# Gates and p's product of a two-block model as split products, with the waits around them reordered

## The chip, the cores and the metric

The kernel runs on one core of one Trainium2 chip. It is written in Bass: each of the five instruction streams (TensorE = PE, VectorE = DVE, ScalarE = ACT, SyncE = SP, GpSimd = POOL, the last unused) is written out by hand, and they meet only through semaphores. The metric is the device time in microseconds (us), the median of several runs; lower is better.

## The reference, cut to what matters

Two blocks run one after the other on x, 256 positions by 2048 channels, in float32. The first has two layers; each projects the normed x to 6668 columns, sends them through three mixers (sliding window attention over 12 heads, a conformer convolution, a gated delta rule), gates the results y and adds `y @ w_out` to x. The second has two layers as well: a pool mixer in layer 0, a recurrent unit (LRU) in layer 1. The parts that the change touches are these:

```
# attention of a layer of the first block, per head h
s = q k^T / 8, masked; p = softmax([s, sink]);  o = p v;  y[0:768] = o * silu(za)
# LRU: uc = causal conv of u over 4 positions, 16 heads of 256 channels
r  = sigmoid(uc_h @ wa_h + ba);  ig = sigmoid(uc_h @ wx_h + bx)
# end of both layers of the second block
x = x + rmsnorm(o) * g_post
gate = sigmoid(rmsnorm(x) @ w_ple_gate);  e = p[i] @ w_ple      # p[i]: 256 x 256
x = x + rmsnorm(e * gate) * g_ple_out
```

## The kernel before

**Weights.** All weights lie in one array in the order of use, in chunks of at most 128 x 2048 float32 (1 MB). `plan()` makes the list. SP loads chunk c into `W[c % 5]` once chunk c - 5 is used up. A chunk named in `SPLIT` is taken apart: ACT copies it, rounded to fp32r, into `WH[s % 4]` (`high`, L991), once the split chunk four before it is used up; DVE writes the rest, W - WH, over the chunk itself as `WL` (`low`, L1658). The inputs are held the same way as an upper and a low part (`HH`, `HL` for the first block's h and y). A split product is three fp32r matmuls: WL by the upper part, WH by the low part, WH by the upper part. In mode "wide" the last two are one matmul of 512 columns, so a k-tile is four matmuls of 256 columns and four of 512. The LRU's gate weights (`lru_w`, eight chunks) and `w_ple_2` (two chunks a layer) are not in `SPLIT`: their products are plain float32 matmuls, straight from `W`.

**Order on the engines.** Each engine walks the same list of chunks. On ACT and DVE a `tick` runs `high(c + 3)` or `low(c + 3)` first and then four `pump`s; PE runs four `pump`s spread over the k-tiles of a chunk. A pump moves every side task (a Python generator) on by one `yield`, so `rest(n)` puts n pumps between two steps of a side task. `group(n)` is n ticks and then a wait for the last chunk of them; `finish` runs a side task to its end. Each engine runs its own stream in order, so a wait holds back all that is behind it. `lag` says how many of the engine's own earlier instructions may still be under way.

**Attention.** It is a side task on PE (L743 ff.), ACT (L1210 ff.) and DVE (L1947 ff.), begun at the start of the projection of za. Heads are taken in three lots q of four: `scores(q)` on PE writes four PSUM banks; on DVE it scales and masks each into `AS`, takes the maxima and signals `mx`; on ACT it takes the exponentials and signals `es`; `weights(q)` on DVE divides by the sum and signals `p`; `turned(q)` transposes three banks on PE, which ACT and DVE copy back to `AS`; last comes `av` (three banks), multiplied by silu(za) into Y on DVE. The four side banks of PSUM go round in a fixed order: `turned(0)` and `turned(1)` write banks that the first three DVE operations of `scores(1)` and `scores(2)` set free. With PE's chunks after the start of attention named Z1 to Z4 (za, pumps 1 to 16), P (17 to 20), A (21 to 24), B (25 to 28), G1 (k-tiles 10 to 13 of y, 29 to 32), G2 (6 to 9, 33 to 36), G3 (14 and 15, 37 to 40), G4, G5, G6 (the same k-tiles for the next 512 output columns, 41 to 52) and G7 (k-tiles 0 to 3), the steps stand at these pumps:

```
              PE   ACT  DVE          after: PE   ACT  DVE
scores(0)     22   26   19                  22   26   22
weights(0)              27                            30
scores(1)     30   34   27 (behind weights) 30   34   30
turned(0)     32   32   29                  32   32   32
weights(1)              35                            38
scores(2)     38   42   35                  38   42   38
turned(1)     40   40   37                  40   40   40
silu(za)           43                            43
weights(2)              43                            46
turned(2)     48   48   45                  47   47   47
av            52        49                  50        50
X back (DMA)       52                            50
```

After B both ACT and DVE leave the side tasks for a moment: DVE scales the last part of Y (`scaled`), ACT and DVE write upper and low parts of y's k-tiles 6 to 9, 14 and 15 (`ysplit`), which G2 and G3 read. Those of k-tiles 0 to 5 come after `finish(att)`.

**End of a layer of the second block.** `out_part(l, 3)` adds the last part of the output product to O in four column groups i; DVE adds (after `low` of the tick), ACT sums the squares, DVE multiplies by g_post. `post(l, n)` then takes the total, ACT the inverse root, and DVE adds O to X in eight operations. On PE, `post` runs four groups of p's product and after each but the first transposes a quarter of X (`turn`), whose copies become the upper and low parts of the next h.

**LRU.** In step n, PE projects z(n) and u(n + 1), then runs `gates(n)`: 16 matmuls of 256 columns over uc, in two halves (r and ig). `conv(n)` on DVE and `first_tap(n)` on ACT make uc as side tasks. Eight chunks of the output product stand between u(3) and `gates(2)`, between u(5) and `gates(4)`, and behind `gates(6)`.

## Time and profile before

| | us |
|---|---|
| median of 3 runs | 2449.18 (2449.09 to 2449.77) |
| profiled execution, whole | 2449.32 |
| its span, first to last instruction | 2447.5 |
| PE busy | 2414.6 (99%) |
| DVE busy | 1657.7 (68%) |
| ACT busy | 1250.9 (51%) |
| mean granted PE clock | 0.997 |
| DMA, mean | 175 GB/s, 48% of the 16 engines |

A line of the timeline reads: start, duration, engine, line, operation, output <- input, shapes, count, and in brackets the engine's idle time before it with what ended it. L421 is the helper `mm`, L991 `high`, L1658 `low`; L977, L1623 and L1627 are the helpers of all other ACT and DVE work. A plain float32 matmul shows as two records. Matmul durations overlap: the time of one is the distance between starts.

### The profile page before, as it was taken

How to read it: one execution, taken by the hardware profiler on the slowest of the kernel's cores; microseconds unless marked ns; L12 is line 12 of the kernel's file. 1: busy time of each engine (PE TensorE's matmuls, PEld its weight loads, DVE VectorE, ACT ScalarE, POOL GpSimd, SP SyncE). 2: the span in 40 equal slices, each digit the busy share in tenths (PEclk: the TensorE clock that was granted, in tenths of full speed). 3: DMA queues.
4: the chain of work that ended last, by engine and by line, in shares of the span. 5: the costliest groups of instructions: out<-in, count | busy, mean ns of one | idle time of the engine just before them, and what ended most of it. 6: DMA issues, size and time to landing. Idle time of an engine off the chain costs nothing.

```text
span 2447.5 us, 34157 instructions
## 1 busy us (share of the span) xinstructions
PE 2414.6 (99%) x14580; PEld 2139.5 (87%) x14580; DVE 1657.7 (68%) x1895; ACT 1250.9 (51%) x1378; POOL 0.2 (0%) x4
## 2 busy tenths in 40 slices
PE   8999999999999999999999999999999999999997
PEld 8999988899999888988888888878888888888876
DVE  5788758557887585667657577565657667667764
ACT  5554256455543565544444344456556465565573
POOL 0000000000000000000000000000000000000000
PEclk9999999999999999999999999999999999999999
DMA  6543223555532335555555555555454555555553
GB/s 235 207 175 137 98 109 130 198 206 199 182 138 90 118 130 198 195 189 189 189 189 189 189 189 189 194 206 191 153 186 179 193 183 189 189 177 185 203 193 121
DMA packets 63977, 428.17 MB, mean 175 GB/s; under 512 B 7121, under 2 KB 7249, under 8 KB 14801
## 3 DMA queue, kind: packets, MB, share of 16 engines
q1 hardware_dynamic: 61280, 414.97, 47.6%
q10 hardware_dynamic: 2544, 11.01, 1.2%
q8 instruction: 115, 1.88, 0.3%
q14 instruction: 38, 0.30, 0.0%
HBM read 421.76 MB, written 4.19 MB: 174 GB/s over the span
## 4 chain that ended last, share of the span: by engine, by line
PE 97%; DVE 1%; ACT 1%; issue 0%; DMA 0%; DVEq 0%; SPq 0%; ACTq 0%
PE PS L421 95%; PE PS L547 1%; PE PS L652 1%; DVE X L1627 0%; PE PS L643 0%; PE PS L785 0%; ACT Q L977 0%; ACT WH L991 0%; PE PS L766 0%; DVE SM L1642 0%; DVE Q L1627 0%; DVE O L1623 0%; DMA W<-in_wall 0%; DVE H L1623 0%; DVE Y L1623 0%
## 5 line engine op out<-in xcount | busy, mean ns | idle before, releaser
L1658 DVE TENSOR_TENSOR WL<-W,WH 128x2048 fp32r<-128x2048 f32 (+2 forms) x392 | 860.4, 2203 | 505.7 <-ACT WH L991 505.3
L991 ACT ACTIVATE WH<-W 128x2048 fp32r<-128x2048 f32 (+2 forms) x392 | 718.0, 1842 | 506.4 <-PE PS L421 421.1
L421 PE MATMUL PS<-H,WH 128*128 128x256 f32 (+1 forms) x4864 | 946.5, 327 | 0.0
L421 PEld LDWEIGHTS PS<-H,WH 128*128 128x128 f32 x4864 | 713.0, 191 | 43.9
L421 PE MATMUL PS<-H,WL 128*128 128x256 f32 x3392 | 558.3, 284 | 7.6 <-DVE H L1627 7.6
L421 PEld LDWEIGHTS PS<-H,WL 128*128 128x128 f32 x3392 | 503.2, 190 | 50.9 <-issue 9.2
L421 PE MATMUL PS<-WH,H 128*128 128x512 f32 (+1 forms) x1280 | 331.1, 379 | 0.0
L421 PEld LDWEIGHTS PS<-WH,H 128*128 128x128 f32 x1280 | 234.1, 188 | 46.1
L421 PE MATMUL PS<-WH,YS 128*128 128x512 f32 x1024 | 273.8, 389 | 0.0
L421 PEld LDWEIGHTS PS<-WH,YS 128*128 128x128 f32 x1024 | 192.2, 188 | 40.0
L421 PE MATMUL PS<-WL,H 128*128 128x512 f32 (+1 forms) x640 | 197.2, 387 | 5.3 <-DVE H L1623 5.3
L977 ACT ACTIVATE Q<-PS 128x512 f32<-128x512 f32 (+2 forms) x142 | 75.3, 577 | 226.5 <-PE PS L421 114.2
L421 PE MATMUL PS<-WL,YS 128*128 128x512 f32 x512 | 158.0, 390 | 1.2 <-DVE YS L1623 1.2
L421 PEld LDWEIGHTS PS<-WL,H 128*128 128x128 f32 x640 | 114.8, 188 | 26.5 <-issue 7.8
L1623 DVE TENSOR_TENSOR Q<-Q,PS 128x512 f32<-128x512 f32 (+1 forms) x106 | 69.3, 680 | 88.8 <-PE PS L421 42.3
L421 PEld LDWEIGHTS PS<-WL,YS 128*128 128x128 f32 x512 | 96.0, 188 | 21.5 <-issue 1.6
L421 PE MATMUL PS<-Q 128*128 128x128 f32 (+1 forms) x960 | 112.6, 281 | 0.0
L421 PEld LDWEIGHTS PS<-Q 128*128 128x128 f32 (+1 forms) x960 | 108.9, 191 | 4.0 <-issue 1.4
L1627 DVE SCALAR_TENSOR_TENSOR QA<-Q,TB,QA 128x256 f32<-128x256 f32 x240 | 107.6, 478 | 0.0
L1627 DVE SCALAR_TENSOR_TENSOR Q<-Q,TB 128x256 f32<-128x256 f32 x206 | 93.7, 492 | 10.1 <-ACT Q L977 9.5
L977 ACT ACTIVATE Q<-Q 128x1024 f32<-128x1024 f32 (+4 forms) x58 | 65.4, 1127 | 59.1 <-DVE Q L1623 40.8
L421 PE MATMUL PS<-D,WH 128*128 128x512 f32 x256 | 69.9, 394 | 0.0
(146 smaller groups left out, 1598.9 us busy)
## 6 DMA issues: line engine op xcount, KB each, us to landing
W<-in_wall SPq DMA_DIRECT2D x374, 1024.0 KB, 4.8
W<-in_wall SPq DMA_DIRECT2D x24, 512.0 KB, 3.5
W<-in_wall SPq DMA_DIRECT2D x8, 536.0 KB, 3.6
X<-in_xT SPq DMA_DIRECT2D x8, 256.0 KB, 5.4
X<-in_x ACTq DMA_DIRECT2D x1, 2048.0 KB, 10.6
xsave<-X ACTq DMA_DIRECT2D x1, 2048.0 KB, 8.3
X<-xsave ACTq DMA_DIRECT2D x1, 2048.0 KB, 11.9
Q<-in_g_post ACTq DMA_DIRECT2D x8, 256.0 KB, 3.4
```

What stands on the lines that cost most here:

```text
L421: return e.matmul(o, l, r, start=start, stop=stop, skip_group_check=True)
L547: o = e.transpose(b[:, 256 * j + 128 * t:256 * j + 128 * t + 128], X[:, t, c:c + 128], ident)
L652: i = e.transpose(b[:, 128 * j:128 * j + 128], TT_[:, us], ident)
L977: e.activation(o, a, f, **k).then_inc(*up(*sig))
L991: e.activation(WH[:, s % NSPL, 0:m], W[:, c % NRAW, 0:m], ACT.Copy).then_inc(*up("hi", c))
L1623: e.tensor_tensor(o, a, b, op).then_inc(*after(sig))
L1627: e.scalar_tensor_tensor(out=o, in0=a, scalar=s, in1=b, op0=op0, op1=op1).then_inc(*after(sig))
L1658: e.tensor_tensor(WL[:, c % NRAW, 0:m], W[:, c % NRAW, 0:m], WH[:, s % NSPL, 0:m].bitcast(F32), ALU.subtract).then_inc(*up("lo", c))
```

## The change

- `w_ple_2` and `lru_w` join `SPLIT`. p's input gets an upper part `PTH` (ACT, `upper_pt`) and a low part `PTL` (DVE, `lower_pt`), both made early in the layer. The gates' input uc gets `UH` (ACT) and `UL` (DVE), one pair of buffers laid over a constant table that is no longer read; `UH` waits for the previous call of gates.
- Attention's steps stand at the pumps of the right half of the table above, and `ysplit(0)` and `ysplit(2)` are done inside it, behind av 1 and av 2.
- In the last part of the output product DVE adds before it runs the next `low` (`group_ahead`), and takes the total ahead of the last multiplication by g_post.
- In `post` DVE runs `lower(i)` ahead of each `low`.

```diff
 NSPL = 4
-SPLIT = ("w_in", "w_vba", "w_out", "w_in_2", "w_out_2", "w_ple_gate_2", "pool_w_2")
+SPLIT = ("w_in", "w_vba", "w_out", "w_in_2", "w_out_2", "w_ple_gate_2", "w_ple_2", "pool_w_2", "lru_w")
 SLOT = 2048
...
         TB = ctx.enter_context(nc.sbuf_tensor("TB", [128, NT], F32))
+        tb_at = nc.sbuf_base - 4 * NT
         SM = ctx.enter_context(nc.sbuf_tensor("SM", [128, 1056], F32))
...
         PT = Q[:, 21760:22272].rearrange("p (k t) -> p k t", k=2)
+        PTL = over("PTL", 21760, [128, 2, 256], F32R)
+        PTH = nc.alloc_sbuf_tensor_at("PTH", [128, 2, 256], F32R, offset=q_at - 4 * 512)
         ZT = Q[:, 8192:10240].rearrange("p (i c) -> p i c", i=8)
...
                tuple(QA[:, 1024 * k:1024 * k + 1024] for k in range(3)))
+        UHL = [nc.alloc_sbuf_tensor_at(n_, [128, 4, 256], F32R, offset=tb_at + 4 * (-(-AT["b_conv_w"] // 8) * 8 + 1024 * k))
+               for k, n_ in enumerate(("UH", "UL"))]
         MIX = QA[:, 0:1024].rearrange("p (j t) -> p j t", j=4)
...
                         x = self.src(kt)
+                        x = x if isinstance(x, tuple) else (x[:, 0], x[:, 1], x) if c in split_no else x
                         if c not in split_no:
...
                         elif self.mode == "wide":
-                            passes = ((lo, x[:, 0]), (hi, x.rearrange("p k t -> p (k t)")))
+                            passes = ((lo, x[0]), (hi, x[2].rearrange("p k t -> p (k t)")))
                         else:
-                            passes = ((lo, x[:, 0]), (hi, x[:, 1]), (hi, x[:, 0]))
+                            passes = ((lo, x[0]), (hi, x[1]), (hi, x[0]))
                         for n_p, (wt, s) in enumerate(passes):
...
                 turned(1)
-                yield from rest(8)
+                yield from rest(7)
                 turned(2)
-                yield from rest(4)
+                yield from rest(3)
                 av = AV.rearrange("p (t d) -> p t d", t=2)
...
                     c = here["c"]
-                    ucv = ucs[n % 2]
-                    w.wait_ge(*to(f"w{c % NRAW}", c))
-                    w.wait_ge(*to("uc_v", n))
+                    hi, lo = (v[:, i, :].rearrange("p (k n) -> p k n", k=8)
+                              for v, i in ((WH, split_no[c] % NSPL), (WL, c % NRAW)))
+                    uh, ul = UHL
+                    w.wait_ge(*to("lo", c))
+                    w.wait_ge(*to("uc_v", "lo", n))
                     g = here["g"]
...
                     for k0 in (0, 4):
-                        wt = W[:, c % NRAW, :].rearrange("p (k n) -> p k n", k=8)[:, k0:k0 + 4, :]
                         for kl in range(2):
-                            for h in range(2):
-                                for j in range(2):
-                                    i = mm(bank(g, k0 // 2 + h)[:, 256 * j:256 * j + 256],
-                                           wt[:, 2 * h + kl, 128 * j:128 * j + 128], ucv[:, 2 * h + kl, :],
-                                           start=(kl == 0 and j == 0), stop=(kl == 1))
+                            for n_p, (wt, s) in enumerate(((lo, uh), (hi, ul), (hi, uh))):
+                                for h in range(2):
+                                    for j in range(2):
+                                        i = mm(bank(g, k0 // 2 + h)[:, 256 * j:256 * j + 256],
+                                               wt[:, k0 + 2 * h + kl, 128 * j:128 * j + 128], s[:, 2 * h + kl, :],
+                                               start=(kl == 0 and n_p == 0 and j == 0), stop=(kl == 1 and n_p == 2))
                         if k0 == 0:
...
                 for i in range(4):
-                    g = Group(lambda kt: PT[:, kt, :], lambda kt: [("pT", l)], 512, "tm", 2)
+                    g = Group(lambda kt: (PTH[:, kt], PTL[:, kt]), lambda kt: [("d_v", "pT", l)], 512, "tm", 2)
                     g.feed(kts=range(2), col=512 * (i % 2), half=None if i == 1 or i == 3 else (l, i))
...
                 act(Y[:, 0:6, :], Y[:, 0:6, :], ACT.Silu, "at_a", l, "za")
-                yield from rest(5)
+                yield from rest(4)
                 turned(2)
-                yield from rest(4)
+                yield from rest(3)
                 w.wait_ge(*to("at_p", l, "turn", 8))
...
+            def upper_pt(l):
+                w.wait_ge(*to("pT", l))
+                act(PTH[:, :, :], PT, ACT.Copy, "u_a", "pT", l)
+
...
                 for g in range(4):
+                    if g == 1:
+                        upper_pt(0)
                     for i in range(2):
...
                             bias=tb("conv_b_2", i), lag=m)
+                    yield from rest(50 if n in (3, 5) else 18)
+                    w.wait_ge(*to("uc_v", n))
+                    if n:
+                        w.wait_ge(*to("chunk", gate_chunk[n - 1]))
+                    act(UHL[0][:, :, :], ucs[n % 2], ACT.Copy, "u_a", "uh", n)
                     yield
...
                 for n in range(8):
+                    if n == 1:
+                        upper_pt(1)
                     if n < 7:
...
                 w.wait_ge(*to("chunk", here["c"] - 1))
+                return here["g"] - 1
+
+            def group_ahead(n):
+
+                for _ in range(n - 1):
+                    tick()
+                w.wait_ge(*to("chunk", here["c"]))
+                here["c"] += 1
+                for _ in range(4):
+                    pump()
+                here["g"] += 1
                 return here["g"] - 1
...
                          *(("at_v", l, "kr") if t else ()), lag=t)
-                yield from rest(4)
+                yield from rest(7)
                 s3 = AS.rearrange("p (h c) -> p h c", h=12)
...
                 weights(2)
-                yield from rest(2)
+                yield
                 turned(2)
-                yield from rest(4)
+                yield from rest(3)
                 for n in range(3):
...
                     w.wait_ge(*to("at_a", l, "za"))
-                    tt(ya, ya, sbank("at", l, "av", n), ALU.mult, "at_v", l, "av", n, lag=n)
+                    tt(ya, ya, sbank("at", l, "av", n), ALU.mult, "at_v", l, "av", n, lag=2 if n else 0)
+                    if n:
+                        ysplit(l, 2 * n - 2, 1)
                 yield
+
+            def ysplit(l, k, lag):
+                w.wait_ge(*to("y_a", l, k))
+                tt(HL[:, k:k + 2, :], Y[:, k:k + 2, :], HH[:, k:k + 2, :].bitcast(F32), ALU.subtract, "y_v", l, k,
+                   lag=lag)
...
-                def ysplit(k, lag):
-                    w.wait_ge(*to("y_a", l, k))
-                    tt(HL[:, k:k + 2, :], Y[:, k:k + 2, :], HH[:, k:k + 2, :].bitcast(F32), ALU.subtract, "y_v", l, k,
-                       lag=lag)
-
...
                 for k in (6, 8):
-                    ysplit(k, k // 2 - 3)
-                ysplit(14, 2)
+                    ysplit(l, k, k // 2 - 3)
+                ysplit(l, 14, 2)
                 for _ in range(6):
...
                 finish(att)
-                for k in (0, 2, 4):
-                    ysplit(k, k // 2)
+                ysplit(l, 4, 1)
                 add_x(0, group(2))
...
+            def lower_pt(l):
+                w.wait_ge(*to("u_a", "pT", l))
+                tt(PTL[:, :, :], PT, PTH[:, :, :].bitcast(F32), ALU.subtract, "d_v", "pT", l)
+
...
                     for i in range(4):
-                        gi = group(2 // halves)
+                        final = g == 3 and hf == halves - 1
+                        if final:
+                            gi = group_ahead(2 // halves)
+                        else:
+                            gi = group(2 // halves)
                         cs = slice(512 * i, 512 * i + 512)
...
                                 tt(O[:, t, cs], O[:, t, cs], bank(gi, t), ALU.add, *(("ev_v", gi) if t else ()), lag=t)
-                        if g == 3 and hf == halves - 1:
+                        if final and i < 3:
+                            low(here["c"] + NSPL - 2)
+                        if final and i == 3:
+                            total(3 + 4 * l)
+                        if final:
                             w.wait_ge(*to("norm_a", "ss", 3 + 4 * l, i, 1))
...
                 for g in range(4):
+                    if g == 1:
+                        lower_pt(0)
                     for i in range(2):
...
                                 *(("uc_v", n) if k == 2 and m == 3 else ()), lag=3 if k else m)
+                    yield from rest(38 if n in (3, 5) else 6)
+                    w.wait_ge(*to("u_a", "uh", n))
+                    tt(UHL[1][:, :, :], ucv, UHL[0][:, :, :].bitcast(F32), ALU.subtract, "uc_v", "lo", n)
...
                 for n in range(8):
+                    if n == 1:
+                        lower_pt(1)
                     if n < 7:
...
             def post(l, n):
-                total(3 + 4 * l)
                 w.wait_ge(*to("norm_a", "rstd", 3 + 4 * l))
...
                             *(("x_v", "mid", l, i) if t else ()), lag=min(2 * i + t, 3))
-                for i in range(4):
-                    tick(again=i in (0, 2))
-                    if i:
-                        lower(n, i - 1)
+                for _ in range(4):
+                    pump()
+                for i in range(3):
+                    lower(n, i)
+                    low(here["c"] + NSPL - 2)
+                    if i < 2:
+                        here["c"] += 1
+                    for _ in range(4):
+                        pump()
                 here["g"] += 4
...
```

## Rows read from the trace of the kernel before

**Rows 1.** The page: engine shares, and the chain of waits by engine
```profile
PE 2414.6 (99%) x14580; PEld 2139.5 (87%) x14580; DVE 1657.7 (68%) x1895; ACT 1250.9 (51%) x1378; POOL 0.2 (0%) x4
...
PE 97%; DVE 1%; ACT 1%; issue 0%; DMA 0%; DVEq 0%; SPq 0%; ACTq 0%
```

**Rows 2.** Waits, of PE: total us, times, longest
```profile
PE PS L547 <- DVE X L1627: 6.4, 2, 5.4
PE PS L421 <- DVE H L1623: 5.3, 4, 1.7
```

**Rows 3.** Groups by form: count | busy us, mean ns | idle
```profile
L421 PE MATMUL PS<-Q,W 128*128 128x256 f32 x256 | 56.5, 379 | 0.0
...
L421 PE MATMUL PS<-W,Q 128*128 128x512 f32 x64 | 28.4, 592 | 0.0
```

**Rows 4.** Timeline, PE, around the first call of gates
```profile
1807.34 1.09 PE L421 MATMUL PS<-H,WH 128*128 128x512 f32 x4
...
1808.27 7.07 PE L421 MATMUL PS<-Q,W 128*128 128x256 f32 x32
...
1815.64 1.08 PE L421 MATMUL PS<-H,WH 128*128 128x512 f32 x4
```

**Rows 5.** Timeline, PE, split product with 256 columns
```profile
398.61 0.64 PE L421 MATMUL PS<-H,WH 128*128 128x256 f32 x4
...
399.33 0.64 PE L421 MATMUL PS<-H,WH 128*128 128x256 f32 x4
```

**Rows 6.** Timeline, DVE, ahead of the first call of gates
```profile
1804.17 2.29 DVE L1658 TENSOR_TENSOR WL<-W,WH 128x2048 fp32r<-128x2048 f32 x1 [1.24 <-ACT WH L991]
```

**Rows 7.** Chain in order of time: start, us, what
```profile
466.59 5.46 PE PS L421 x24
...
1636.06 3.44 PE PS L421 x8
```

**Rows 8.** Timeline, ends of layers 0 and 1 of the second block
```profile
1628.96 5.39 DVE L1627 SCALAR_TENSOR_TENSOR X<-O,SM,X 128x512 f32<-128x512 f32 x8 [0.60 <-ACT SM L977]
...
2329.40 7.03 PE L421 MATMUL PS<-W,Q 128*128 128x512 f32 x16
...
2331.05 1.28 DVE L1623 TENSOR_TENSOR O<-O,PS 128x512 f32<-128x512 f32 x2
...
2335.96 5.39 DVE L1627 SCALAR_TENSOR_TENSOR X<-O,SM,X 128x512 f32<-128x512 f32 x8 [0.60 <-ACT SM L977]
```

**Rows 9.** Timeline, DVE, attention of layer 0
```profile
402.46 1.83 DVE L1623 TENSOR_TENSOR Q<-Q,SM 128x512 f32<-128x512 f32 x2
...
405.05 1.95 DVE L1627 SCALAR_TENSOR_TENSOR Q<-PS,TB 128x384 f32<-128x384 f32 x4 [0.76 <-PE PS L421]
...
409.42 0.69 DVE L1623 TENSOR_TENSOR Y<-PS,RBT 128x512 f32<-128x512 f32 x1
```

**Rows 10.** Timeline, ACT, attention of layer 0
```profile
403.69 1.89 ACT L991 ACTIVATE WH<-W 128x2048 fp32r<-128x2048 f32 x1
...
425.01 0.39 ACT L977 ACTIVATE Q<-Q,SM 128x128 f32<-128x128 f32 x1
...
431.62 1.04 ACT L991 ACTIVATE WH<-W 128x1024 fp32r<-128x1024 f32 x1
```

**Rows 11.** Timeline, PE, attention of layer 0
```profile
408.61 1.47 PE L785 MATMUL PS<-TB,Q 128*128 128x128 f32 x12
...
411.06 0.70 PE L421 MATMUL PS<-WL,H 128*128 128x512 f32 x2 [0.98 <-DVE H L1623]
...
418.06 1.68 PE L421 MATMUL PS<-Q 64*128 64x128 f32 x16
...
443.67 0.70 PE L421 MATMUL PS<-WL,H 128*128 128x512 f32 x2 [1.67 <-DVE H L1623]
```

**Rows 12.** Windows: busy us of PE, PEld, DVE, ACT, POOL; granted clock; DMA
```profile
1728.33:1733.76 5.43, 0.00 (x1) 0.00 (x1) 3.61 (x7) 3.44 (x8) 0.00 (x0) 0.89 0.59 193
1733.76:1739.20 5.44, 5.44 (x26) 5.44 (x27) 4.52 (x9) 4.01 (x9) 0.00 (x0) 0.50 0.00 0
```

## The prediction

> **What bounds the kernel now.** I read the page's engine shares and the chain of waits first [rows 1]: TensorE (PE) is busy 2414.6 of 2447.5 us and holds 97% of the chain. So time comes or goes in two ways only: less or more work on PE, or PE standing still. What PE stands still for is in the list of waits [rows 2]: 5.3 us over four waits for the low parts of y (two per attention layer), 6.4 us over two waits for X at the ends of the second block's layers (5.4 at the end of its first, so 1.0 in its second). VectorE (68%) and ScalarE (51%) matter only where PE waits for one of them. The profiled execution took 2449.32 us around its span of 2447.5; the median of the three runs is 2449.18, so a difference worked out in the trace is taken off either alike.
>
> **Part 1, the gates (128 plain products become 384 split ones).** The 128 plain matmuls show as 256 records of 256 columns [rows 3]: a plain one takes two records. One call of gates, 16 matmuls, starts at 1808.27; the wide products after it are in step again at 1815.64, and their first four narrow matmuls took 0.47 (a wide k-tile is 1.40, its four 512-column matmuls 0.93, from 1807.34 to 1808.27 [rows 4]). So the call costs 1815.64 - 0.47 - 1808.27 = 6.90 us. After, it is 48 matmuls of 256 columns. These have a price: six of them take 0.72, from 398.61 to 399.33 [rows 5], 0.12 each, so 5.76. Saved: 1.14 a call, 9.1 in eight. The parts' making is off PE: per call one more high (1.9, ScalarE), one more low (2.3, VectorE), UH (1.1) and UL (1.2); VectorE was idle a third of the time, and a weight chunk's low is made three chunks (some 17 us) ahead. Only UL is near its reader. conv(n)'s 29th pump issues it. For n = 1, 6, 7 the product is nine chunks after the start, for 3 and 5 the longer rest puts it two chunks ahead too (2 and 4 have more): 5 us of cover. For n = 0 there are eight chunks, and the 29th pump is the first of the eighth tick, behind low(c+3). That low began at 1804.17 [rows 6]; now that the gates' weights take one of the four WH slots, its high waits for a chunk that ends 5.60 before the gates, at 1802.67; with 2.1 for that and 2.3 for itself the low ends near 1807.1, UL near 1808.3, where PE wants it at 1808.27: 0.2 us of wait. I take 8.9 saved. Bounds: 9.1, and 7 if UL ends one low (2.3) later.
>
> **Part 2, p's product.** Eight plain matmul records (one group of four) are 3.44 us; 24 split ones of 512 columns 5.46, so twelve are 2.73 [rows 7]: 0.71 saved in each of eight groups, 5.7. But PE must have X for its first turn after two groups, and gets there 1.42 sooner. Layer 1: X's first slice was ready at 2335.96 + 1.42 = 2337.38 [rows 8], PE stood 1.0. The edit takes two things out of that chain: low ahead of O's last addition (PE's last product before it ends by 2329.6, just past the start of p's products at 2329.40; the addition began at 2331.05: 1.4) and, since total goes ahead of the gain's multiplication, the wait of the norm for it; but those multiplications (1.3) still stand ahead of X's on VectorE, so only 0.6 of them comes off. X is there near 2335.4, PE at 2334.9: it stands 0.6, and the first turn is 1.96 earlier. Layer 0: no low was in the way; X moves from 1628.96 + 1.42 [rows 8] to some 1629.9, PE arrives at 1629.2 and stands 0.7: 0.7 gained. The other two groups give 1.42 in each layer. The first gate chunk's low now stands behind X's eight operations (5.4) and one lower (1.7): it ends near 2343.4, PE comes at 2343.5. That just fits. Sum 1.96 + 0.7 + 2.8 = 5.5; I take 5.4. Bounds 5.7 + 1.0, and 3 if that low is late by 1.2 in each layer.
>
> **Part 3, attention.** This is where I part with the wording "lined up". VectorE runs low(c+3) first in each tick and then its four pumps, in order, and any wait blocks what is behind. Pumps count from the start of attention; names of chunks as in the section on the kernel. Before, VectorE had weights(0) and scores(1) at pump 27 (tick B), then stood until PE's scores at pump 30; scaled Y came at 409.42, the low parts after it, and PE stood until 411.06; low(G4) ran only after them [rows 9, 11]. After, they are at pump 30, in tick G1, behind scaled Y, three ysplits and low(G4). Step by step, in the clock of before:
> - Y and the low parts: B ends at 401.2; ScalarE has y's upper parts done when it begins high(G4) at 403.69 [rows 10], VectorE the low parts at 404.7. PE's wait of 1.1 for them goes.
> - low(G4) needs its high, which ScalarE makes from 403.69 to 405.58, behind its exponentials: low ends 407.85 (2.2 of its own time). weights(0), 2.26 (1.83 and two small steps), ends 410.1. scores(1) starts 410.2; its four operations take 1.95, 0.49 each, its reductions bring the whole to 4.3 (405.05 to 409.32) [rows 9].
> - PE comes to turned(0) at 408.6 and needs weights(0) and, for its three PSUM banks, the first three operations of scores(1): 410.8, 411.2, 411.7. It ends at 412.2, where G2 started at 411.06 before (in step: 411.1) [rows 11]. **Later by 1.1.**
> - ScalarE: G5's high to 414.4, exponentials of scores(1) (3.85) to 418.35, G6's high to 419.4; low(G6) to 420.65; weights(1) to 422.9; scores(2) from S = 423.0. PE: G2 (5.44), a k-tile (1.36), scores(2) (1.8 with its gaps; 1.68 in the row), a k-tile: 422.2. It needs S + 1.5 for its third bank, so turned(1) ends at 425.0; before, 422.5. **Later by 2.5 in all.**
> - weights(2) moves from pump 43 to 46, so behind low(G8), which waits for a high that stands behind the exponentials and za's Silu: S + 4.3, exponentials from 427.5, high(G8) 6.6 later (425.01 to 431.62 [rows 10]) at 434.1 to 435.2, low (1.2) 436.4, weights(2) 438.65. PE, with turned(2) one pump sooner, comes at 425.0 + 5.44 + 4.08 = 434.5 and **stands 4.1 us**.
> - av two pumps sooner puts a k-tile (1.36) behind it, and ysplit(0) follows av 1, so the wait of 1.7 before G7 [rows 2] goes. From turned(2) at 438.65: 1.35 + 1.36 + 1.36 + 4.4 (av) + 1.36 gives G7 at 448.7 against 443.75 (443.67 in the trace, set in step).
> So waits of 2.9 a layer go and 7.8 come: +4.95 a layer, +9.9 in two. Below, the bound is a gain of all four old waits, 2 x 2.9 = 5.8; above, 7 a layer, if ScalarE is a further high (1.9) late. I take +9.9, since the chain from S to weights(2) is 15.6 us of single durations while PE has only 11.5 us from S to turned(2).
> The rest (upper_pt, lower_pt, 0.6 and 0.7 each, two of either) lies under products; no DMA is added. The return of X is issued near 441.6 and is wanted near 457. The stall of 5.43 at 1728.33 isn't touched.
>
> **Sum.** -8.9 - 5.4 + 9.9 = -4.4: 2449.32 - 4.4 = 2444.9 for the profiled execution, 2444.8 for the median.
>
> **Rivals.**
> - The clock falls in attention's longest stall. In the idle 5.43 us before 1733.76 the granted clock averages 0.89, so it fell to 0.50 (1.2 of 2.4 GHz) some 4.2 us after PE's last work, and stayed for 5.44 us of work [rows 12]: 2.7 us lost. An idle time of 1.67 (the longest of rows 2's four) did nothing. Mine of 4.1 lies at the edge. One fall 2447.5, one per layer 2450.2. Chance 0.17. The Trainium skill, "TensorE: Matmul & The Clock Gate", section on HAM oscillation, says that waits for data between bursts can put the array back to half rate, so that each next burst starts cold; the rows at 1733.76 agree, and no row shows it for 4.1 us.
> - **Slower:** the same mechanism at two places in each layer, the stalls at turned(0) (2.2 us) and turned(2) (4.1). Four falls at 2.7 are 10.9: 2455.7. It decides from 9.3 us, so from four falls. For it: nothing bounds the idle time that does it between 1.67 and 5.43. Against: 2.2 is near 1.67. Chance 0.10.
> - Attention costs half or nothing: if weights get in before the low, or ScalarE runs ahead of where I put it. 2435 to 2440. Chance 0.17.
> - The steps do line up and all four old waits go: 2449.2 - 14.3 - 5.8 = 2429. For it: each pump number is now the same on the engines that exchange data there. Against: a pump number orders only pumps, the lows stand before them. Chance 0.11.
>
> **Numbers.** My own case has 0.45, 2442.5 to 2447. A measurement can tell about 0.2%, 4.9 us: faster is under 2444.3. I give 0.18 of my case's 0.45 to that side, for it lies 0.5 us from the border. Faster 0.18 + 0.17 + 0.11 = 0.46; same 0.27 + 0.17 = 0.44; slower 0.10. The range, 2434 to 2453, leaves out the last rival and the slower one.
>
> **What would show it.** Right: Q,W and W,Q records gone from the groups; a gates call at 5.76 us; in each attention layer a PE wait near 4 us that ends with weights(2), on VectorE behind a 1024-wide low, and shorter ones before turned(0) and turned(1); no wait for the low parts of y; X's waits at 0.6 to 0.7 us. Wrong: PE waits for UL at several gates; a granted clock of 0.50 after 438; attention's stretch from B's end to G7 no longer than its 42.3 us of before.

## The result, and the profile after

The changed kernel took 2460.59 us (median of 5 runs, 2456.33 to 2461.91) against 2449.18 before: 1.0041 of the time, 95% interval 1.0029 to 1.0052, so 11.4 us slower. The prediction was 2444.8, with 2434 to 2453 as its range: it said faster or the same, and lies 16 us off. The profiled execution took 2461.91 around a span of 2459.9, 12.4 more than the span before.

The page's shares, against [rows 1]; PE is busy 2.1 us less and idle 14.5 us more:

```profile
PE 2412.5 (98%) x14740; PEld 2151.3 (87%) x14740; DVE 1693.4 (69%) x1917; ACT 1282.5 (52%) x1400; POOL 0.2 (0%) x4
```

PE's waits (total us, times, longest), against [rows 2]. Left out are the wait at the kernel's start (8.1 us, 7.6 before) and one for YS (1.2 in both):

```profile
PE PS L791 <- DVE Q L1644: 7.8, 2, 3.9
PE PS L553 <- DVE X L1648: 6.2, 3, 5.4
PE PS L791 <- DVE Q L1648: 5.9, 4, 2.1
PE PS L426 <- issue: 5.8, 3, 2.3
```

The four waits for y's low parts are gone. L791 is turned: PE stands before turned(0), (1) and (2) in both attention layers, 13.7 us. The row "issue" hides a name: its three places are all the first matmul of a call of gates. Here is the first of them, with the VectorE rows ahead of it (timeline: start, us, what, idle before):

```profile
1876.62 0.92 PE L426 MATMUL PS<-UH,WL 128*128 128x256 f32 x4 [2.34 <-issue]
```

```profile
1869.75 1.23 DVE L1644 TENSOR_TENSOR YS<-Q,YS 128x1024 fp32r<-128x1024 f32 x1
1870.89 4.49 DVE L1679 TENSOR_TENSOR WL<-W,WH 128x2048 fp32r<-128x2048 f32 x2
1875.30 1.22 DVE L1644 TENSOR_TENSOR UL<-Q,UH 128x1024 fp32r<-128x1024 f32 x1
```

UL ends at 1876.52 and PE begins at 1876.62: PE waits for UL, which stands behind two low parts of weights. At gates 6 and 7 UL also ends 0.1 us before PE begins; at gates 6 two low parts stand ahead of it, at gates 7 one and an addition to O.

In attention (VectorE, layer 0), against [rows 9], the steps stand where the prediction put them, low(G4) at 406.31 ahead of weights(0), low(G8) at 437.11 ahead of weights(2):

```profile
406.31 2.29 DVE L1679 TENSOR_TENSOR WL<-W,WH 128x2048 fp32r<-128x2048 f32 x1 [0.95 <-ACT WH L999]
...
408.96 1.83 DVE L1644 TENSOR_TENSOR Q<-Q,SM 128x512 f32<-128x512 f32 x2
410.89 1.49 DVE L1648 SCALAR_TENSOR_TENSOR Q<-PS,TB 128x384 f32<-128x384 f32 x3
...
437.11 1.23 DVE L1679 TENSOR_TENSOR WL<-W,WH 128x1024 fp32r<-128x1024 f32 x1 [4.96 <-ACT WH L999]
...
438.68 1.83 DVE L1644 TENSOR_TENSOR Q<-Q,SM 128x512 f32<-128x512 f32 x2
```

What isn't in the waits is the clock: behind some stalls PE works for a while at 0.50, the lower of its two levels (1.2 of 2.4 GHz), which I call a fall. Below are windows of 6 us from the end of each stall of 1.6 us or more (the stalls, in order: 2.13, 3.92, 2.13, 3.91, 2.34, 1.62, 1.89). The granted clock, a mean over the window, is the number behind POOL's. The wait of 5.43 for X, which stands in both kernels, is left out; the clock behind it is 0.53 before and 0.58 after.

```profile
411.59:417.59 6.00, 6.00 (x26) 5.11 (x27) 5.79 (x11) 4.79 (x13) 0.00 (x0) 0.72 0.12 47
440.56:446.56 6.00, 6.00 (x29) 5.21 (x31) 1.38 (x2) 2.24 (x2) 0.00 (x0) 0.77 0.11 23
910.00:916.00 6.00, 6.00 (x26) 5.10 (x27) 5.79 (x11) 4.79 (x13) 0.00 (x0) 0.72 0.12 50
939.00:945.00 6.00, 6.00 (x20) 5.26 (x21) 1.38 (x2) 1.12 (x2) 0.00 (x0) 0.50 0.00 0
1876.62:1882.62 6.00, 6.00 (x38) 6.00 (x39) 6.00 (x6) 3.23 (x6) 0.00 (x0) 0.72 0.28 116
2220.37:2226.37 6.00, 6.00 (x49) 6.00 (x50) 6.00 (x6) 4.16 (x6) 0.00 (x0) 1.00 0.37 154
2271.78:2277.78 6.00, 6.00 (x38) 6.00 (x38) 6.00 (x5) 2.35 (x4) 0.00 (x0) 0.72 0.36 150
```

PE counts as busy in them, so no list of waits shows this loss. A window at 0.72 loses 0.28 x 6 = 1.7 us, one at 0.50 loses 3.0. In the rows it shows as slower work. Twelve transposes of turned(2) in layer 0 took 2.82 us, where twelve like them took 1.47 in turned(0) of before [rows 11]:

```profile
440.56 2.82 PE L791 MATMUL PS<-TB,Q 128*128 128x128 f32 x12 [3.92 <-DVE Q L1644]
```

The sum along PE, after less before:

- start 0.7 (the first wait is 8.1 instead of 7.6; it differs as much between runs of one kernel);
- attention, layer 0: waits 6.87 less the old 2.65, 4.2, and clock (0.28 + 0.23) x 6 = 3.1: 7.3 (measured 7.5 from B's end to G7); layer 1: 4.2 + (0.28 + 0.50) x 6 = 8.9 (measured 9.0);
- p's product and the end of its layer: -2.2 in layer 0, -3.4 in layer 1;
- gates: eight calls of 5.76 instead of 6.90, -9.1; waits 5.85; clock 3.4. Sum +0.1, measured +0.7.

The measured stretches add up to 12.3 of the 12.4. The same sum from the waits and clocks alone gives 11.4: it is 0.2 short in attention's first layer, 0.1 in its second, and 0.6 at the gates, and I did not trace those.

### The profile page after: what moved, and what is told of

Read it like the earlier page. It is cut to its first block, busy times and chain, and to the rows that moved or that the text cites. A ratio compares the mean times of both kernels' runs of the same rounds, so it can differ in the third digit from the quotient of the medians.

```text
span 2459.9 us, 34557 instructions
## 1 busy us (share of the span) xinstructions
PE 2412.5 (98%) x14740; PEld 2151.3 (87%) x14740; DVE 1693.4 (69%) x1917; ACT 1282.5 (52%) x1400; POOL 0.2 (0%) x4
## 4 chain that ended last, share of the span: by engine, by line
PE 89%; DVE 5%; ACT 3%; issue 2%; DMA 0%; DVEq 0%; SPq 0%; ACTq 0%
PE PS L426 87%; DVE WL L1679 1%; ACT Q L985 1%; ACT WH L999 1%; DVE Q L1644 1%; PE PS L553 1%; DVE Q L1648 1%; PE PS L658 1%; PE PS L791 1%; DVE X L1648 0%; ACT L985 0%; DVE O L1644 0%; PE PS L649 0%; ACT QA L985 0%; DVE Q L2285 0%
## 5 line engine op out<-in xcount | busy, mean ns | idle before, releaser
L1679 DVE TENSOR_TENSOR WL<-W,WH 128x2048 fp32r<-128x2048 f32 (+2 forms) x404 | 888.3, 2206 | 502.2 <-ACT WH L999 501.2
L999 ACT ACTIVATE WH<-W 128x2048 fp32r<-128x2048 f32 (+2 forms) x404 | 741.2, 1844 | 497.6 <-PE PS L426 424.0
```

The costliest lines, as they stand in the source:

```text
L999: e.activation(WH[:, s % NSPL, 0:m], W[:, c % NRAW, 0:m], ACT.Copy).then_inc(*up("hi", c))
L1679: e.tensor_tensor(WL[:, c % NRAW, 0:m], W[:, c % NRAW, 0:m], WH[:, s % NSPL, 0:m].bitcast(F32), ALU.subtract).then_inc(*up("lo", c))
```

## Experiments

Each was timed in five rounds beside the kernel before, whose median was 2449.0 to 2449.5 in each set. "Less than the changed kernel" means less than 2460.84, its median in run 1; only runs 2, 4 and 8 were timed in one set with that.

**1. The changed kernel again.** 

> The changed kernel as it is, beside the others on the same chip. All theories: 2460.6, between 2456 and 2462, whose spread (4 to 5 us) I expect to follow how often the clock falls behind the stalls of 2 us or less: in a fast execution fewer of the five or six short stalls have a stretch at 0.50 behind them. If the spread has another cause, the profile's stretches look as before and the time is still spread.

 Measured 2460.84 (2460.14 to 2461.22), so this time nearly without the spread. The trace has the same stalls, but at turned(0) of layer 1 the clock stood at 1.00 behind the same 2.13 us (windows as above):

```profile
910.69:916.69 6.00, 6.00 (x33) 5.16 (x34) 5.79 (x11) 4.80 (x13) 0.00 (x0) 1.00 0.10 39
938.33:944.33 6.00, 6.00 (x21) 5.28 (x22) 1.38 (x2) 1.12 (x2) 0.00 (x0) 0.53 0.00 0
```

**2. Attention taken back.**
```diff
-                yield from rest(7)
+                yield from rest(4)
                 s3 = AS.rearrange("p (h c) -> p h c", h=12)
...
                 weights(2)
-                yield
+                yield from rest(2)
```
and so on, all attention steps and y's low parts as before. 

> The changed kernel with its attention steps back at their old places and y's low parts again in one go. My theory: the lined-up steps cost about 8.2 us a layer, of which 4.9 are TensorE's idle time before turned(0), (1) and (2) less the old waits, and 3.3 come from falls of the granted clock to 0.50 behind the 2.1 and the 3.9 us stall. Both go: 16 to 17 us less than the changed kernel, about 2444. Rival A, only the waits are attention's doing and the rest comes from elsewhere: 10 us less, 2451. Rival B, the attention cost nothing and the gates and the reorder lost it all: within 2 us of the changed kernel, 2459.

 Measured 2442.16, 0.9970 of before (0.9959 to 0.9981): 18.7 less than the changed kernel. My theory, 2 us beyond its number: the wait at gates 7 also came down to 1.57, with no fall behind it.

**3. Attention alone, on the kernel before.** 

> The kernel before with only attention's new steps. My theory: what taking them out of the changed kernel gave back (18.4 us, 16.5 of it by the two traces) comes on here: 16 to 18 us more, 2465 to 2467. Rival, attention's cost depends on the other two parts (for instance on the clock's state they leave): 10 us more, the bare waits, 2459.

 Measured 2464.41, 1.0062 (1.0050 to 1.0075): 14.9 more: nearer to the 16 to 18 expected than to the rival's 10, and its interval (12 to 18) leaves the rival out. Here too the clock stayed at 1.00 behind one of the two stalls of 2.13.

**4. Only weights(2) taken back.**
```diff
-                yield from rest(6)
+                yield from rest(3)
                 weights(2)
-                yield
+                yield from rest(4)
                 turned(2)
```


> The changed kernel with only weights(2) on VectorE back at its old place, three pumps earlier, and turned(2) left at 47. My theory: the 3.9 us stall before turned(2) comes from weights(2) standing behind the low part of G8; it goes to below 0.5 us, and the fall of the clock behind it (about 1.5 us) goes too: 5.4 us a layer, 10 to 11 in all, about 2450. Rival A, the clock falls from the 2.1 us stall of turned(0) and only keeps low: 8 us less, 2452.5. Rival B, ScalarE's high part of G8 (on which the low part waits) is what is late, and turned(2) waits for the low part through av instead: less than 3 us, 2457 or more.

 Measured 2447.37, 0.9991 (0.9982 to 1.0000): 13.5 less than the changed kernel, where my theory had 10 to 11. The rows for turned(2) are gone from the waits of PE, those for turned(0) and (1) stay:

```profile
PE PS L553 <- DVE X L1648: 6.2, 3, 5.4
PE PS L791 <- DVE Q L1648: 5.9, 4, 2.1
PE PS L426 <- issue: 5.9, 3, 2.3
```

So weights(2) behind low(G8) is the costliest single edit: 7.8 us of waits, and most of the rest is clock (0.52 and 0.53 over 6 us behind the two stalls in run 1's trace, 5.7). I had priced a fall at 1.5 here; in most profiles the windows behind this stall stand near 0.52, which is 2.9.

**5. The counterpart: only weights(0), weights(1) and scores taken back.** 

> The changed kernel with scores(1), weights(0) and weights(1) on VectorE three pumps earlier, at their old places, and weights(2) left behind the low part of G8 (the counterpart of the run that took only weights(2) back). My theory: the stalls at turned(0) and turned(1) (2.1 and 0.8) and the fall of the clock behind the first (about 1.4) go, a wait of 1.0 for y's low parts comes back: 3.3 us a layer, 6.6 in all, and the stall at turned(2) stays near 4 us, since it hangs on the chain from scores(2) over the exponentials and G8's high to weights(2), which comes forward by as much as PE does: 2454. Rival A, that chain is tied to the weight chunks (ScalarE's high of G8 waits for its own turn in the order of chunks), so the stall at turned(2) grows by part of what was gained before it: less than 3 us in all, 2458 or more. Rival B, the stall at turned(2) needs the earlier delay and shrinks below 2 us without it: 12 us or more, 2449 or less.

 Measured 2452.15, 1.0010 (1.0001 to 1.0019): 8.7 less than the changed kernel, nearest to my theory (6.6) and 2.1 beyond it. The stall at turned(2) was unchanged, 3.93, though turned(2) began at 436.64 instead of 440.56: the chain from scores(2) to weights(2) moves with PE. The profiled execution (2448.98) is one of the shorter ones of this kernel; it has no fall at the gates, so its trace is not that of the median. Runs 4 and 5 together, 22.2, equal what goes from attention in all (run 2, and run 6 for the tail: 18.7 + 3.8 = 22.5).

**6. Only attention's tail, on the kernel before** (turned(2), av and y's low parts two pumps sooner, VectorE's weights and scores at their old places). 

> The kernel before with only the tail of attention's new steps: turned(2), av and the low parts of y two pumps sooner on all engines, but scores, weights(0) and weights(2) on VectorE at their old places. My theory: no step stands behind a low that waits for its high, so no wait is added, and the second wait for y's low parts (1.7 us a layer) goes: 3.5 us less, 2446. Rival A, turned(2) one pump sooner meets PE before weights(2) is done and the gain is lost: 2449. Rival B, av two pumps sooner makes the chunks behind it late: 1 us more than before.

 Measured 2445.51, 0.9986 (0.9977 to 0.9995): 3.8 less, my theory (3.5). Of the waits for H in [rows 2] this is left:

```profile
PE PS L426 <- DVE H L1633: 2.0, 2, 1.0
```

**7. The gates alone, on the kernel before.** 

> The kernel before with the gates as split products and nothing else of the change. My theory: eight calls save 1.14 each, 9.1; PE waits for UL at gates 1, 6 and 7 for about 6.5 us less the 0.9 that these calls' idle time held before, and loses 3.4 to two falls of the clock: 0 to 1 us more than before, 2449.5. Rival A, the falls belong to the whole change and don't come here: 3 us less than before, 2446. Rival B, the gates alone save what I predicted (8.9) and the waits come from the reorder or from p's product: 2440.

 Measured 2446.13, 0.9987 (0.9978 to 0.9996): 3.3 less, rival A's number. With the 4.8 us of waits below, the 9.1 saved would leave 4.3; the missing 1.0 was not traced. The three waits are there, shorter, with the clock at 1.00 behind each (windows from their ends; the stalls were 1.61, 1.62 and 1.54):

```profile
1860.32:1866.32 6.00, 6.00 (x50) 6.00 (x51) 6.00 (x6) 4.16 (x6) 0.00 (x0) 1.00 0.38 157
2202.58:2208.58 6.00, 6.00 (x49) 6.00 (x50) 6.00 (x6) 4.16 (x6) 0.00 (x0) 1.00 0.41 167
2253.65:2259.65 6.00, 6.00 (x50) 6.00 (x51) 6.00 (x5) 4.16 (x7) 0.00 (x0) 1.00 0.42 168
```

**8. UH and UL four pumps earlier, in the changed kernel** (rest(50)/(18) to 46/14 on ScalarE, rest(38)/(6) to 34/2 on VectorE). 

> The changed kernel with u's high and low part (UH, UL) made four pumps earlier on ScalarE and VectorE. My theory: VectorE runs one to two chunks behind TensorE where gates 1, 6 and 7 begin, so UL comes 2.3, 1.6 and 1.9 us late, and the clock falls twice behind these stalls; four pumps are about 4 us of VectorE's time, so the stalls go with the falls: 9 to 10 us less, about 2451. Rival A, the stalls go but the clock's loss there has another cause: 6.5 us less, 2454. Rival B, gates are held by what VectorE must do in all (lows, scan and UL), so that an earlier UL only delays the low part of the weights by as much: within 2 us of the changed kernel.

 Measured 2458.30: 2.5 less than the changed kernel, close to rival B's number (within 2); my theory fell in this form. At gates 1 ScalarE shows why. UH began at the same time as before (1869.69; u itself is ready only then), but now ahead of a high part instead of behind it:

```profile
1869.69 1.06 ACT L985 ACTIVATE UH<-Q 128x1024 fp32r<-128x1024 f32 x1 [2.73 <-DVE Q L1648]
1870.66 5.50 ACT L999 ACTIVATE WH<-W 128x2048 fp32r<-128x2048 f32 x3
```

and on VectorE the one low part still ahead of UL waits for that high:

```profile
1872.59 2.29 DVE L1679 TENSOR_TENSOR WL<-W,WH 128x2048 fp32r<-128x2048 f32 x1 [1.60 <-ACT WH L999]
1874.80 1.22 DVE L1644 TENSOR_TENSOR UL<-Q,UH 128x1024 fp32r<-128x1024 f32 x1
```

At gates 7 UL did come early, at 2265.6, and PE stood 1.75 us all the same, now until VectorE had added to O. That is rival B's mechanism:

```profile
2272.23 0.71 PE L426 MATMUL PS<-UH,WL 128*128 128x256 f32 x4 [1.75 <-DVE O L1644]
```

**9. UL alone five pumps earlier, UH where it was.**
```diff
-                    yield from rest(38 if n in (3, 5) else 6)
+                    yield from rest(33 if n in (3, 5) else 1)
                     w.wait_ge(*to("u_a", "uh", n))
```


> The changed kernel with UL five pumps earlier on VectorE and UH left where it is on ScalarE. With UH earlier too, UL came only 0.5 us sooner at gates 1, since UH pushed ScalarE's high part back and the low part ahead of UL waited 1.6 us for it. My theory: what makes UL late is its place behind two or three low parts of weights that nobody waits for yet (4.5 us at gates 1 and 6, 2.3 and O's addition at gates 7); ahead of them it is done at 1872.1 where PE wants it at 1874.3, and the stalls of 2.3, 1.6 and 1.9 go with both falls: 9 us less than the changed kernel, 2451. Rival A, VectorE has no slack there, so the lows that UL passes come late themselves and PE waits 1.2 us each time for them: 6 us less, 2454.5. Rival B, no gain as before (within 2.5 us of 2460).

 Measured 2453.31, 1.0016 (1.0008 to 1.0025): 7.5 less than the changed kernel, between my number and rival A's, and both mechanisms are in it. The stalls and their falls are gone; what stands in their place is small, and its first row is rival A's, a low part of weights that UL has passed (PE, gates 1):

```profile
1872.04 0.74 PE L426 MATMUL PS<-UH,WL 128*128 128x256 f32 x4 [0.28 <-DVE WL L1679]
...
1878.93 0.71 PE L426 MATMUL PS<-H,WL 128*128 128x256 f32 x4 [0.88 <-DVE Q L1644]
```

**10. The same edit on the gates alone.** 

> The kernel before with the gates as split products and UL five pumps earlier on VectorE. My theory: the prediction's term for the gates (8.9 less) was right in its arithmetic and failed only in UL's place, so that here 8 to 9 us come off: 2441. Alone the split gave 3.3, with PE's waits for UL of 1.61, 1.62 and 1.54, 4.8 in all, and no fall of the clock. Rival, the split costs something beside the waits: the same 4.8 come back but no more than 7 in all, 2442.5 or above.

 Measured 2441.57, 0.9968 (0.9956 to 0.9981): 7.7 less, a little under my 8 to 9, of the 9.1 that the records of [rows 3] to [rows 5] give; its trace has 1.5 us of new waits of the 0.88 kind, two of them. 9.1 less 1.5 is 7.6, so the arithmetic of the split holds.

**11. p's second pair of parts behind gates 1 instead of ahead** (`if n == 1` to `if n == 2` before upper_pt(1) and lower_pt(1), in run 2's kernel). 

> The changed kernel with attention's old steps, and with the two operations that make the second layer's parts of p one product later (behind the gates of n = 1 instead of ahead). Alone the gates wait 1.61 us for UL at n = 1, in the whole change 2.35 with a fall of the clock behind it. My theory: the 0.7 of difference is the low part of p, which stands ahead of UL on VectorE, and the fall comes from that: the stall is 1.6 again, the clock stays at 1.00, and the time is 2.0 to 2.5 less than the same kernel without the move (2442.2): 2440. Rival, the two parts of p are hidden there and the stall has grown for another reason: 2442.

 Measured 2440.03 against 2442.16 without the move. The stall is 1.60 and the clock behind it 1.00:

```profile
1858.19 0.71 PE L426 MATMUL PS<-UH,WL 128*128 128x256 f32 x4 [1.60 <-issue]
```

So work that the prediction had called hidden under products lengthened the wait for UL from 1.60 to 2.36 (the stall in run 2's trace), and with that brought the fall of the clock: 2.1 us. But it isn't the operation that my expectation names. The edit moves two, 0.63 us on ScalarE (PTH) and 0.69 on VectorE (PTL), and the traces tell them apart. In run 2:

```profile
1813.95 0.63 ACT L985 ACTIVATE PTH<-Q 128x512 fp32r<-128x512 f32 x1
1814.49 1.90 ACT L999 ACTIVATE WH<-W 128x2048 fp32r<-128x2048 f32 x1
1814.62 0.69 DVE L1644 TENSOR_TENSOR PTL<-Q,PTH 128x512 fp32r<-128x512 f32 x1 [2.40 <-ACT PTH L985]
1816.43 2.29 DVE L1679 TENSOR_TENSOR WL<-W,WH 128x2048 fp32r<-128x2048 f32 x1 [1.11 <-ACT WH L999]
```

and in run 11, whose gates 0 begin 0.60 earlier:

```profile
1813.15 1.93 ACT L999 ACTIVATE WH<-W 128x2048 fp32r<-128x2048 f32 x1
1815.12 2.29 DVE L1679 TENSOR_TENSOR WL<-W,WH 128x2048 fp32r<-128x2048 f32 x1 [3.50 <-ACT WH L999]
```

VectorE has 3.5 us idle there. PTL fits in, with 1.11 of idle time left behind it. What comes 0.7 later is ScalarE's high, behind PTH; VectorE's low waits for it, and the same 0.7 is still there at UL, 40 us on (1858.20 against 1856.87, less the 0.60 of offset).

This is one way in which the parts interact. Alone they give -3.3, -5.9 and +14.9, +5.7 in all, together +11.4. Of the 5.7 between, these are 2.1. Another 2.0 stand at gates 7, where the wait is 1.57 without a fall in run 2 and 1.89 with one in the whole change; why attention's steps lengthen it was not traced. The rest stays open.

**12. p's product and the reorder alone.** 

> The kernel before with p's product split and the end of each block's layer reordered, nothing else. My theory, which is the prediction's term: 5.4 us less, 2443.7. Rival, it costs something at the first gates (the low part of the first chunk behind X's operations): 3 us less, 2446.

 Measured 2443.59, 0.9977 (0.9967 to 0.9986): 5.9 less, my theory. How much of it is the split and how much the reorder was not timed.

**13. The best of it:** runs 6, 9 and 12 in one kernel. 

> The changed kernel with scores, weights(0) and weights(2) on VectorE at their old places and UL five pumps earlier. My theory: the four parts add: 5.9 for p's product (measured alone), 8.8 for the gates, 3.5 for attention's tail, less 0.3 for the wait of gates 1: 2449.4 - 17.9 = 2431.5. Rival A, attention's tail gives nothing: 2435. Rival B, VectorE, which now makes more lows earlier, is late at another place: 2436 or more.

 Measured 2433.84 (2433.17 to 2435.11), 0.9937 of before (0.9923 to 0.9950): 15.5 us less than before and 27.0 less than the changed kernel. That lies between my 2431.5 and rival A's 2435, but rival A is not what happened: the wait before G7 is gone here too. PE's waits behind the start:

```profile
PE PS L553 <- DVE X L1648: 6.2, 3, 5.4
PE PS L426 <- DVE H L1644: 2.0, 2, 1.0
PE PS L426 <- DVE Q L1644: 1.7, 2, 0.9
PE PS L426 <- DVE YS L1644: 1.2, 1, 1.2
PE PS L426 <- DVE WL L1679: 0.3, 1, 0.3
```

Its parts, measured one by one, give 5.9 + 7.7 + 3.8 = 17.4, so 1.9 are missing. **14.** I looked for them in p's second pair: 

> The best version so far (p's product, gates with UL early, attention's tail; 2433.8) with p's second pair of parts one product later. My theory: only the wait of 0.28 at the gates of n = 1 goes: within 0.6 us of 2433.8. Rival, the 2 us that this version lacks to the sum of its parts are there: 2432 or less.

 Measured 2434.04: they aren't there. One candidate is in the traces. Behind the wait of 5.44 for X, which no part touches, the clock over 6 us was 0.53 in the kernel before, 0.75, 0.76 and 0.70 in the profiles of runs 6, 10 and 12, and 0.58 in run 13's. So each single part had 0.9 to 1.3 us there that it did not earn, run 13 only 0.3. Whether the medians hold the same luck isn't shown, and what the 1.9 are stays open.

## Why the prediction was wrong, point by point

- **The step that failed first: the fall of the clock.** The prediction read that an idle time of 1.67 did nothing and one of 5.43 did it [rows 2, 12], took its own stalls of 2.2 and 4.1 as harmless, and gave falls 0.27 in two rivals. The slower rival's mechanism is the one that came: falls at turned(0) and turned(2) in both layers. Even it was too low (2455.7), since it had no stalls at the gates. Their size, 2.7 each, was fair for turned(2) (1.4 to 3.0) and high for turned(0) (1.7). In the trace: 7.8 us in attention, 3.4 at the gates. That all four came was in part chance: in run 1 one of the stalls at turned(0) had 1.00 behind it.
- **The second step: "5 us of cover" for UL.** I counted pumps and chunks: UL issued one or two chunks ahead of its reader, a weight's low "three chunks (some 17 us) ahead". That is distance in the program, not in time. VectorE runs late there, and the trace of before showed it. Gates 1 began at 1860.06, and VectorE was at two low parts of later chunks until 1860.63:

```profile
1856.14 4.49 DVE L1658 TENSOR_TENSOR WL<-W,WH 128x2048 fp32r<-128x2048 f32 x2
...
1861.43 0.69 DVE L1623 TENSOR_TENSOR Q<-Q,PS 128x512 f32<-128x512 f32 x1 [0.81 <-issue]
```

  UL's 1.22 behind them end 1.8 us after the start of gates 1. I read VectorE's rows only at n = 0 [rows 6], where I expected 0.2 us of wait and there is none. At gates 6 and 7 the same rows of before end at 2206.60 and 2257.15, for gates that began at 2206.03 and 2256.50, which gives 1.8 and 1.9. Run 7 measured 1.61, 1.62 and 1.54, and run 9, which moves UL alone, shows that they are UL's. The prediction's bound for this part, 7 us saved at worst, allowed for one late low at one call, not at three. Waits and falls at the gates cost 9.2 us where it had 0.2.
- **"Lies under products" for upper_pt(1) and lower_pt(1)** was the third: PE doesn't wait for them, but UL comes later by them (run 11). The way goes over ScalarE: upper_pt(1) makes a high 0.7 late, VectorE's low waits for that high, and UL stands behind the lows. lower_pt(1) itself fills idle time of VectorE.
- Neither of the first two would have left the stated range alone. 2444.8 with attention's waits as found (-1.5) and its falls (7.8) is 2451; with the gates' waits and falls instead it is 2452. Both together give 2460.
- **Attention's waits were right but for turned(1).** Predicted 2.2, 1.5 and 4.1 with 2.9 of old waits going; found 2.13, 0.82, 3.92 and 2.65: 8.4 for both layers instead of 9.9. Which step stands behind which low was right in every place (runs 4 and 5).
- **p's product was right**: 5.4 predicted, 5.9 measured alone; first turn in layer 1 1.96 earlier predicted, 2.05 found (13.65 of offset against 15.70 at the start of p's products); the low of the first gate chunk did not come late. X's waits were 0.36 and 0.38, where 0.7 and 0.6 were predicted.
- **The price of a gates call was right**: 5.76, no stall at n = 0.

The sum, corrected: 2449.3 - 4.4 (forecast) - 1.5 (attention's waits) + 7.8 (clock) + 9.05 (gates: waits 5.85 and clock 3.4, less the 0.2 foreseen) + 0.7 (start) = 2461.0, against 2461.9 in the profiled execution. The measured terms are read from the trace that they explain, so that the sum comes out proves little; that they are causes is shown by runs 2, 4, 5, 9 and 11.

## What to carry to other kernels

Where an edit adds an operation to an in-order engine, read that engine's rows at every place where its result is wanted, and compare its clock time with the consumer's: issue order says nothing of lead. Do the same for what that engine waits for: 0.63 us on ScalarE was enough to make a result of VectorE 0.7 late, 40 us later. A step that is "lined up" by number stands behind whatever that engine runs ahead of its numbered steps, and waits with it. And price a new stall of PE by its idle time and by the granted clock behind it; the second never shows in a list of waits, and here the falls cost 11.2 us beside 14.3 us of waits.

## What the runs showed of the hardware that I had not expected

Over the 16 profiles of this case, PE's stalls between 0.9 and 1.75 us (73 of them, after the start) all have a granted clock of 1.00 in the 6 us behind them. Of 22 stalls from 1.84 to 2.36 us, 16 have 0.72 to 0.74 there and 6 have 1.00. All 12 of 3.9 us have 0.50 to 0.77, all 16 of 5.4 us 0.53 to 0.76. In the middle group the same stall at the same place falls in one execution and not in another: gates 1 with 2.34 us idle stood at 0.72 in the changed kernel, and in run 5's profile, with 2.33, at 1.00:

```profile
1866.82:1872.82 6.00, 6.00 (x50) 6.00 (x51) 6.00 (x6) 3.45 (x6) 0.00 (x0) 1.00 0.32 130
2209.08:2215.08 6.00, 6.00 (x49) 6.00 (x50) 6.00 (x6) 4.16 (x6) 0.00 (x0) 1.00 0.39 160
2260.51:2266.51 6.00, 6.00 (x50) 6.00 (x51) 6.00 (x5) 3.82 (x7) 0.00 (x0) 1.00 0.38 161
```

So idle time alone doesn't decide it. The timed executions of a kernel with such stalls can spread (2448.70 to 2453.77 in run 5), and the spread goes with the clock. In run 5 the four executions at 2448.7 to 2450.3 have a mean granted clock of 0.996 over their span, the seven at 2452.1 to 2453.8 one of 0.993 or 0.994. In the first timing of the changed kernel the two at 2456.3 and 2456.7 have 0.994 and 0.995, the three at 2460.6 to 2461.9 have 0.992. In run 1 all five have 0.992 and lie within 1.1 us. Which stalls fell in the executions that have no profile isn't recorded. The Trainium skill, "TensorE: Matmul & The Clock Gate", section on the HAM clock gate, says that the slow stretch at a kernel's start varies from run to run with the phase of the chip's observation; the middle group here varies from execution to execution behind stalls. That this has the same cause is not shown by any run here.
